# Expert weights loaded in 1 MB halves, and another order of work where the second block begins

## The chip, the cores and the metric

The kernel runs on one core of a Trainium2 chip. The metric is device time in microseconds of one execution; lower is better. Inputs and outputs are fp32.

## The reference

Two blocks follow each other on 256 tokens of width 1024. The first ends in a mixture of 32 experts, of which each token uses two; the second is two layers, each of which begins with an RMS norm and a wide projection. What matters here:

```python
def expert_block(args):                       # for each of the 32 experts
    xb, e = args
    return (jax.nn.silu(xb @ w1[e]) * (xb @ w3[e])) @ w2[e]   # 1024 -> 512 -> 1024
...
x = x + g2[:, None] * y                       # y: weighted sum over experts, by token
x = rmsnorm(x, final_g)                       # end of the first block
...
for layer in range(2):                        # second block
    h = rmsnorm_2(x, norm_w)
    proj = jnp.matmul(h, w_in)                # then attention, retention, mLSTM
    ...
    x = x + jnp.matmul(y, w_out)
return rmsnorm_2(x, final_norm_w)
```

## The kernel before

**Experts.** Experts are worked in 16 pairs (`NP`). The two experts of a pair sit side by side on TensorE, each in 64 of its columns, so one pass over a 512-wide row of weights is one matmul of either expert. A pair takes six loads of 2 MB, issued by SP in the order w1, w1, w3, w3, w2, w2. They go round eight slots of 2 MB (`ring` has six, `more` has two). SP waits before each load until its slot is free: a slot of w1 or w3 is given back by `s_up`, which TensorE raises after all eight rows of the pair's w1 or w3; a slot of w2 by `s_down` after the whole w2. TensorE, in `experts_pe`, waits for whole loads (`arrival`). Per pair it multiplies w1 (L924), w3 (L924), gathers tokens for the next pairs (L881), transposes the weights of tokens and the gated product (L888, L937), adds the pair before to the sum (`scatter_pe`, L901), and multiplies w2 in two halves of 512 columns (L953). ScalarE and VectorE split each result of w2 into a rounded part `ygH` (L1000) and the rest `ygL` (L1055); after the last pair VectorE adds the sum to `xT` (`add_dve`, L1030).

**The second block.** Its weights come as 44 units of 1 MB (22 a layer; one of them, `U_ROWS`, of 512 KB), in four places `raw0` to `raw3`. A unit is multiplied as three fp32r products: ScalarE rounds it to `hi` (L1228), VectorE makes `lo = raw - hi` (L1234), and the input x is split likewise into `HH` (ScalarE, L1674) and `HL` (VectorE, L1971). Each product is HH·hi, HL·hi, HH·lo (L1288). `PIECES` lists the parts of the units in the order of splitting; `high(l, u, i)` and `low(l, u, i)` work it off up to part i of unit u. The first two units of a layer are multiplied together, row by row of the eight rows k (`pair`), each row as soon as its split is there; after row 5 and after row 6 TensorE sums squares for two norms (`stats`, L1318, from squares by ScalarE, L1685 and L1687). The norms' roots and reciprocals (L1582, L1989 to L1999) then stand before everything that reads the projections (L2009 on).

**Order.** Every engine's order is the order in which the code is written; there is no scheduler. Units 0 to 3 and the late constants are issued by SP behind the last expert load, each when its slot is free. A branch for tokens beyond 64 an expert (`overflow`) stands between the experts and the second block; it isn't taken.

Of the kernel before, what the change touches and what calls it, by code (L numbers as in the profile page):

```python
# [32 lines left out]
for _n, _w in (("ident", 128), ("ones", 128), ("one", 256), ("iota", 64), ("low", 128), ("iotam", 32), ("bd", 128), ("negd", 384),  # L33
# [16 lines left out]
PIECES = ([(u, i) for i in range(4) for u in (0, 1)] + [(U_ROWS, 0)] + [(u, i) for u in range(3, U_OUT) for i in range(2)]  # L50
          + [(u, i) for v in (18, 20) for i in range(2) for u in (v, v + 1)])
POOLED = tuple(n for n, (u, i) in enumerate(PIECES) if i == 1 and u in (4, 7, 10, 13))


def build(nc, p, out):
    pe, act, dve, pool, sp = nc.tensor, nc.scalar, nc.vector, nc.gpsimd, nc.sync
    with ExitStack() as ctx:
# [77 lines left out]
        for e in range(0, NE, 2):  # L135
            stream += [piece(p[w][x]) for w in ("expert_w1", "expert_w3") for x in (e, e + 1)]
            stream += [p["expert_w2"][x].rearrange("p (k n) -> p k n", k=4) for x in (e, e + 1)]
# [3 lines left out]
        turns_of = [[n for n in range(len(stream)) if slot_of[n] == i] for i in range(NS)]  # L141
        s_ring = [sem(f"s_ring{i}") for i in range(NS)]

# [9 lines left out]
        def arrival(n):  # L153
            return s_ring[slot_of[n]], 16 * (turns_of[slot_of[n]].index(n) + 1)
# [6 lines left out]
        s_mod, s_mrow, s_fma, s_turn, s_modc, s_half = (sem("s_" + n) for n in ("mod", "mrow", "fma", "turn", "modc", "half"))  # L161
        s_spl, s_proj, s_fill, s_xp, s_cv, s_conv, s_gv, s_ln, s_lnroot, s_sig, s_a, s_aa, s_lru = (
            sem("s_" + n) for n in ("spl", "proj", "fill", "xp", "cv", "conv", "gv", "ln", "lnroot", "sig", "a", "aa", "lru"))
        s_gr, s_gu, s_scan, s_sgu, s_xres = (sem("s_" + n) for n in ("gr", "gu", "scan", "sgu", "xres"))
# [54 lines left out]
        def freed(n):  # L219
# [9 lines left out]
            return (s_up, 2 * q + 1 + r // 2) if r < 4 else (s_down, 2 * q + 2)  # L229
# [8 lines left out]
        def first_sp():  # L238
# [3 lines left out]
            for n in range(FIRST):  # L242
# [4 lines left out]
                if n == ADA[3]:  # L247
                    sp.dma_start(place(W_IN[0])[:, 4:8, :], stream[W_IN[0]][:, 4:8, :]).then_inc(s_half, 16)
# [3 lines left out]

        def stream_sp(first, last):
            for n in range(first, last):
                held = [m for m in turns_of[slot_of[n]] if m < n]
                if held:
                    sp.wait_ge(*freed(held[-1]))
                elif slot_of[n] == 7:
                    sp.wait_ge(s_proj, 18)
                sp.dma_start(place(n), stream[n]).then_inc(s_ring[slot_of[n]], 16)  # L260

# [65 lines left out]
        def mixer_pe():  # L327
# [50 lines left out]
            pe.wait_ge(s_half, 16)  # L378
# [86 lines left out]
            project(14, W_OUT[0], 0, yT, y_ready, 0, (s_gu, 2))  # L465
            project(15, W_OUT[0], 2, yT, None, 0, (s_gu, 4))
# [35 lines left out]
        def mixer_act():  # L502
# [52 lines left out]
            for u, dst, signal in ((8, gr, s_gr), (10, gu, s_gu)):  # L555
# [71 lines left out]
        def mixer_dve():  # L627
# [80 lines left out]
            for j in range(4):  # L708
# [5 lines left out]
                dve.wait_ge(s_gu, j + 1)  # L714
# [191 lines left out]
        def experts_pe(first, last):  # L906
            for n in range(first, last):
                q, o = n // 2, 128 * (n % 2)

                for i in range(2):  # L910
# [33 lines left out]
                for a in range(2):  # L944
# [4 lines left out]
                    for f in range(4):  # L949
                        for x in range(2):  # L950
                            if a == 0 and f == 0:
                                pe.wait_ge(*arrival(at[x]))
                            t = pe.matmul(bank[5 + a][64 * x:64 * x + 64, :], aT[:, f, 64 * x:64 * x + 64],  # L953
                                          place(at[x])[:, f, 512 * a:512 * a + 512], start=f == 0, stop=f == 3)
# [3 lines left out]
        def gathered_act(q, a, ps):  # L958
            act.wait_ge(s_gath, 4 * q + 2 * a + 1)
            if q >= 2:  # L960
                act.wait_ge(s_up, 4 * (q - 1))
# [5 lines left out]
        def gathered_dve(q, a, ps):  # L967
            dve.wait_ge(s_gath, 4 * q + 2 * a + 2)
            if q >= 2:
                dve.wait_ge(s_up, 4 * (q - 1))  # L970
# [5 lines left out]
        def experts_act(first, last, high=None):  # L976
            for n in range(first, last):
                act.wait_ge(s_up, 2 * n + 1)
# [15 lines left out]
                for a in range(2):  # L994
# [6 lines left out]
                    if n == NP - 1:  # L1001
                        high(0, 1, 2 * a + 1)
# [30 lines left out]
        def experts_dve(first, last, low=None):  # L1033
            for n in range(first, last):
# [3 lines left out]
                dve.wait_ge(s_up, 2 * n + 2)  # L1038
# [13 lines left out]
                for a in range(2):  # L1052
# [4 lines left out]
                    if n == NP - 1 and a == 0:  # L1057
                        low(0, 1, 1)
# [1132 lines left out]
        for a in range(4):  # L2191
            add_dve(a)
# [117 lines left out]
```

## Time and profile before

| | |
|---|---|
| device time, median of 3 runs | 954.54 us (954.53 to 956.31) |
| the profiled execution | 954.87 us, its span 953.1 us |
| PE busy | 878.9 us, 92% of the span |
| DMA in the span | 291.42 MB, mean 306 GB/s |
| HBM read | 289.52 MB |
| q1 (all weight loads) | 24480 packets, 74.1% of 16 engines' span |
| expert loads | 96 of 2 MB, 27 us from issue to landing |

The page divides the span into 40 slices. In slices 8 to 24 DMA moves 403 to 428 GB/s; from slice 25 on it moves 45 to 221. PE is busy nearly everywhere, and VectorE and ScalarE, light in the experts, rise to 7 or 8 tenths and 5 to 7 tenths behind them. Busy shares alone don't say which of them sets the pace; the chain of waits does.

### The profile page before, as it was taken

How to read it: one execution, taken by the hardware profiler on the slowest of the kernel's cores; microseconds unless marked ns; L12 is line 12 of the kernel's file. 1: busy time of each engine (PE TensorE's matmuls, PEld its weight loads, DVE VectorE, ACT ScalarE, POOL GpSimd, SP SyncE). 2: the span in 40 equal slices, each digit the busy share in tenths (PEclk: the TensorE clock that was granted, in tenths of full speed). 3: DMA queues.
4: the chain of work that ended last, by engine and by line, in shares of the span. 5: the costliest groups of instructions: out<-in, count | busy, mean ns of one | idle time of the engine just before them, and what ended most of it. 6: DMA issues, size and time to landing. Idle time of an engine off the chain costs nothing.

```text
span 953.1 us, 12730 instructions
## 1 busy us (share of the span) xinstructions
PE 878.9 (92%) x5340; PEld 579.0 (61%) x5340; DVE 415.0 (44%) x780; ACT 310.3 (33%) x564; POOL 36.7 (4%) x23
## 2 busy tenths in 40 slices
PE   4999999999989898898988988889999998999995
PEld 2668874444334443344433433788889898888985
DVE  4096951111111111011110110687887858788772
ACT  3362141111011111111111111657256565725662
POOL 0001000000000000000000000011110001111000
PEclk9899999999999999999999999999999999999998
DMA  9999889999999999999999999152333236233321
GB/s 381 425 427 428 321 313 403 428 428 427 428 427 428 427 427 428 427 428 426 428 428 428 428 427 423 45 221 89 134 133 133 99 145 221 89 134 133 133 89 45
DMA packets 24538, 291.42 MB, mean 306 GB/s; under 512 B 2720, under 2 KB 2976, under 8 KB 4000
## 3 DMA queue, kind: packets, MB, share of 16 engines
q1 hardware_dynamic: 24480, 290.58, 74.1%
q8 instruction: 44, 0.72, 0.3%
q14 instruction: 14, 0.11, 0.0%
HBM read 289.52 MB, written 1.05 MB: 305 GB/s over the span
## 4 chain that ended last, share of the span: by engine, by line
PE 54%; DMA 25%; DVE 14%; ACT 5%; issue 2%; SPq 1%; DVEq 0%; ACTq 0%
DMA ring<-in_expert_w 19%; PE bank L1288 15%; PE bank L924 14%; PE bank L953 7%; PE bank L345 4%; DMA more<-in_expert_w 3%; DVE lo L1234 3%; PE bank L881 2%; DMA ring<-in_ada_w 2%; DVE X L315 2%; PE bank L901 2%; PE bank L360 2%; PE bank L387 1%; PE bank L1318 1%; ACT hi L1228 1%
## 5 line engine op out<-in xcount | busy, mean ns | idle before, releaser
L924 PE MATMUL bank<-ring,xg 128*64 128x512 f32 x768 | 236.9, 607 | 21.5 <-DMA ring<-in_expert_w 20.5
L924 PEld LDWEIGHTS bank<-ring,xg 128*64 128x64 f32 x768 | 73.3, 140 | 142.7 <-issue 109.0
L1288 PE MATMUL bank<-HH,hi 128*128 128x256 f32 x432 | 129.1, 299 | 11.4 <-DVE lo L1234 9.1
L924 PE MATMUL bank<-more,xg 128*64 128x512 f32 x256 | 117.1, 608 | 8.1 <-DMA more<-in_expert_w 8.1
L1288 PE MATMUL bank<-HL,hi 128*128 128x256 f32 x432 | 123.3, 286 | 0.0
L1288 PE MATMUL bank<-HH,lo 128*128 128x256 f32 x432 | 123.2, 285 | 0.0
L1042 DVE TENSOR_TENSOR X<-X,bank 128x512 f32<-128x512 f32 x16 | 11.0, 687 | 237.5 <-PE bank L924 237.5
L953 PE MATMUL bank<-ring,X 128*64 128x512 f32 x384 | 113.3, 595 | 0.0
L1288 PEld LDWEIGHTS bank<-HH,hi 128*128 128x128 f32 x432 | 83.9, 194 | 18.6 <-issue 10.2
L1234 DVE TENSOR_TENSOR lo<-raw,hi 128x1024 fp32r<-128x1024 f32 (+1 forms) x86 | 93.1, 1118 | 2.3 <-ACT hi L1228 2.3
L1228 ACT ACTIVATE hi<-raw 128x1024 fp32r<-128x1024 f32 (+1 forms) x94 | 87.0, 975 | 11.2 <-DMA raw<-in_units 11.1
L1288 PEld LDWEIGHTS bank<-HL,hi 128*128 128x128 f32 x432 | 84.0, 195 | 1.1 <-issue 1.0
L1288 PEld LDWEIGHTS bank<-HH,lo 128*128 128x128 f32 x432 | 83.9, 194 | 0.0
L1055 DVE SCALAR_TENSOR_TENSOR ygL<-bank,small,ygH 128x512 fp32r<-128x512 f32 x32 | 24.0, 751 | 131.7 <-ACT ygH L1000 131.7
L924 PEld LDWEIGHTS bank<-more,xg 128*64 128x64 f32 x256 | 34.9, 140 | 49.8 <-issue 37.3
L953 PEld LDWEIGHTS bank<-ring,X 128*64 128x64 f32 x384 | 34.5, 137 | 49.6 <-issue 48.0
L1000 ACT ACTIVATE ygH<-bank,small 128x512 fp32r<-128x512 f32 x32 | 22.0, 687 | 119.1 <-PE bank L953 119.1
L964 ACT ACTIVATE xg<-bank,modc 128x256 f32<-128x256 f32 x32 | 13.4, 470 | 140.4 <-PE bank L881 140.4
L953 PE MATMUL bank<-more,X 128*64 128x512 f32 x128 | 56.6, 595 | 0.7 <-ACT X L993 0.7
L1234 POOL TENSOR_TENSOR lo<-raw,hi 128x1024 fp32r<-128x1024 f32 x8 | 22.5, 2816 | 739.6 <-ACT hi L1228 739.6
L981 ACT ACTIVATE X<-bank 128x512 f32<-128x512 f32 x16 | 9.6, 597 | 110.6 <-PE bank L924 110.6
L1288 PE MATMUL bank<-YH,hi 128*128 128x256 f32 x128 | 37.6, 294 | 2.8 <-DVE lo L1234 2.4
(334 smaller groups left out, 1457.2 us busy)
## 6 DMA issues: line engine op xcount, KB each, us to landing
ring<-in_expert_w SPq DMA_DIRECT2D x72, 2048.0 KB, 27.1
more<-in_expert_w SPq DMA_DIRECT2D x24, 2048.0 KB, 26.9
raw<-in_units SPq DMA_DIRECT2D x42, 1024.0 KB, 4.8
ring<-in_ada_w SPq DMA_DIRECT2D x10, 2048.0 KB, 20.0
ring<-in_w_in SPq DMA_DIRECT2D x3, 2048.0 KB, 33.4
more<-in_ada_w SPq DMA_DIRECT2D x2, 2048.0 KB, 28.1
ring<-in_w_out SPq DMA_DIRECT2D x2, 2048.0 KB, 19.6
ring<-in_w_in SPq DMA_DIRECT2D x2, 1024.0 KB, 22.1
```

The lines of the kernel that those rows point to most:

```text
L315: dve.scalar_tensor_tensor(a, w[:, k, :], cs[:, k:k + 1], a, ALU.mult, ALU.add).then_inc(s_fma, 1)
L345: t = pe.matmul(ps[:, T * j:T * j + T], w[:, k, 128 * (first + j):128 * (first + j) + 128], rhs[:, k, :], start=k == 0, stop=k == 7)
L360: t = pe.matmul(bank[4 + u][:, T * j:T * j + T], w[:, k, 256 * u + 128 * j:256 * u + 128 * j + 128], hT[:, k, :], start=k == 0 and j == 0, ...
L881: t = pe.matmul(ps[:, T * k:T * k + T], part(ht[:, i, d:d + 128]), part(Pm[q % 2][:, i, :]), start=j == 0, stop=j == 3)
L901: t = pe.matmul(bank[ACC[a]][:, T * k:T * k + T], part(y[:, d:d + 128]), part(PT[n % 2][:, :]), start=n == 0 and k == 0 and j == 0, stop=n ...
L924: t = pe.matmul(bank[3 + i][64 * x:64 * x + 64, :], xg[q % 2][:, k, o + 64 * x:o + 64 * x + 64], place(at[x])[:, k, :], start=k == 0, stop ...
L953: t = pe.matmul(bank[5 + a][64 * x:64 * x + 64, :], aT[:, f, 64 * x:64 * x + 64], place(at[x])[:, f, 512 * a:512 * a + 512], start=f == 0, ...
L1000: act.activation(part(ygH[:, 512 * a:512 * a + 512]), bank[5 + a][:, :], ACT.Copy, scale=weight[n % 2]).then_inc(s_ygh, 1)
L1055: dve.scalar_tensor_tensor(part(ygL[:, h]), bank[5 + a][:, :], weight[n % 2], ygH[:, h], ALU.mult, ALU.subtract).then_inc(s_ygl, 1)
L1228: act.activation(part(hi), src, ACT.Copy).then_inc(s_hi, 1)
L1234: e.tensor_tensor(part(lo), src, hi, ALU.subtract).then_inc(signal, 1)
L1288: t = pe.matmul(ps[:, T * j:T * j + T], part(st), part(mv), start=first and a == 0, stop=last and a == 2, skip_group_check=True)
```

## The change

1. Each expert load is cut into two halves of 1 MB, four of the eight rows each (for w2: one half of the 512-column halves, for which w2 is laid out anew on the host). The halves of a pair's two experts are issued alternately: a0, b0, a1, b1. Each half has its own semaphore, TensorE waits for it alone, and raises `s_up` after each four rows and `s_down` after each half of w2, so each half slot is given back by itself.
2. Rows 0 and 1 of units 0 and 1 of the first layer are no longer split. They are multiplied once in plain fp32, raw weights by `yT`, a scaled copy of x.
3. No split of a unit is made between the last evictions of the experts. The additions to `xT`, the splits of x and the splits of the units' rows 2 to 7 are interleaved row by row (`residual_act`, `residual_dve`), ahead of the branch; the splits of x's rows 0 and 1 come last. The squares are made behind all that.

The core of the diff:

```diff
+PIECES = [(l, u, i) for l in range(2) for u, i in
+          [(u, i) for i in range(0 if l else 1, 4) for u in (0, 1)] + ...
-        def freed(n):
+        def freed(n, half=1):
-            return (s_up, 2 * q + 1 + r // 2) if r < 4 else (s_down, 2 * q + 2)
+            return (s_up, 4 * q + 1 + 2 * (r // 2) + half) if r < 4 else (s_down, 2 * q + 1 + half)
+        def experts_sp(first, last):
+            for n in range(first, last):
+                for i in range(3):
+                    for half in range(2):
+                        for m in (first_load(n) + 2 * i, first_load(n) + 2 * i + 1):
+                            slot_free(m, half)
+                            h = slice(4 * half, 4 * half + 4)
+                            sp.dma_start(place(m)[:, h, :], stream[m][:, h, :]).then_inc((s_more if half else s_ring)[slot_of[m]], 16)
...
-                            if k == 0:
-                                pe.wait_ge(*arrival(at[x]))
+                            if k % 4 == 0:
+                                pe.wait_ge(*arrival(at[x], k // 4))
-                    t.then_inc(s_up, 1)
+                        if k % 4 == 3:
+                            t.then_inc(s_up, 1)
...
-                    if n == NP - 1:
-                        high(0, 1, 2 * a + 1)
...
-                    if n == NP - 1 and a == 0:
-                        low(0, 1, 1)
...
+            def whole(l, u, k):
+                return l == 0 and u < 2 and k < 2
+            def whole_of(k):
+                return act.activation(yT[:, k, :], xT[:, k, :], ACT.Copy, scale=gw[:, k:k + 1])
+            def residual_act():
+                act.wait_ge(s_gw, 1)
+                act.wait_ge(s_down, 2 * NP)
+                high(0, 1, 1)
+                act.wait_ge(s_add, 2)
+                for k in range(2):
+                    whole_of(k).then_inc(s_fin, 1)
+                for k in range(2, 8, 2):
+                    act.wait_ge(s_add, k + 2)
+                    x_high(0, k)
+                    x_high(0, k + 1)
+                    if k < 6:
+                        high(0, 1, k // 2 + 1)
+                x_high(0, 0)
+                x_high(0, 1)
+            def residual_dve():
+                add_dve(0)
+                for k in range(2, 8, 2):
+                    add_dve(k // 2)
+                    low(0, 1, k // 2)
+                    x_low(0, k)
+                    x_low(0, k + 1)
+                x_low(0, 0)
+                x_low(0, 1)
...
+                    if whole(l, u, k):
+                        return pe.matmul(ps[:, T * j:T * j + T], v3(raw[U % 4][:, :], 8)[:, k, 128 * j:128 * j + 128], yT[:, k, :], ...)
...
-                    x_high(0, k)
-                    x_high(0, k + 1)
                     act.activation(squares[:, k:k + 2, :], xT[:, k:k + 2, :], ACT.Square).then_inc(s_sqx, 1)
```

On SP's queue the loads of pair 0 stood like this before, each with the semaphore that it waits for:

```order
L260 DMA ring<-in_expert_w1 128x4096 [waits s_fma]
L260 DMA more<-in_expert_w1 128x4096 [waits s_fma]
L260 DMA ring<-in_expert_w3 128x4096 [waits s_proj]
L260 DMA ring<-in_expert_w3 128x4096 [waits s_fma]
L260 DMA more<-in_expert_w2 128x4096 [waits s_proj]
L260 DMA ring<-in_expert_w2 128x4096 [waits s_proj]
```

In the changed kernel the same place, and the first loads of pair 1 behind the read of `longest`:

```order
L280 DMA ring<-in_expert_w1 128x2048 [waits s_fma]
L280 DMA more<-in_expert_w1 128x2048 [waits s_fma]
L280 DMA ring<-in_expert_w1 128x2048 [waits s_fma]
L280 DMA more<-in_expert_w1 128x2048 [waits s_fma]
L280 DMA ring<-in_expert_w3 128x2048 [waits s_proj]
...
L2248 TENSOR_LOAD longest [waits s_pos]
L2248 ISA x2
L280 DMA ring<-in_expert_w1 128x2048 [waits s_mod] x4
L280 DMA ring<-in_expert_w3 128x2048 [waits s_up]
```

Every load became two of half the width, and the second half of the first expert now stands behind the first half of the second.

On ScalarE, from the last results of the experts (`bank5`, `bank6`) on, before:

```order
L1000 ACTIVATE ygH<-bank5,small 128x512
L1228 ACTIVATE hi0<-raw0 128x512
L1228 ACTIVATE hi1<-raw1 128x512
L1228 ACTIVATE hi0<-raw0 128x512
L1228 ACTIVATE hi1<-raw1 128x512
L1000 ACTIVATE ygH<-bank6,small 128x512
```

And behind the branch, where the squares are made, before:

```order
L1674 ACTIVATE HH<-xT,small 128x256 x2
L1685 ACTIVATE scr<-xT 128x512
L1674 ACTIVATE HH<-xT,small 128x256 x2
L1685 ACTIVATE scr<-xT 128x512
L1674 ACTIVATE HH<-xT,small 128x256 x2
L1685 ACTIVATE scr<-xT 128x512
L1674 ACTIVATE HH<-xT,small 128x256 x2
L1685 ACTIVATE scr<-xT 128x512
L1687 ACTIVATE scr<-xT,cols 128x256 x8
L1228 ACTIVATE hi2<-raw2 128x1024
L1582 ACT_TABLE_LOAD
L1582 ACTIVATE rt<-bank7,small 128x256
```

In the changed kernel the same stretch behind the branch:

```order
L1759 ACTIVATE scr<-xT 128x512 x4
L1761 ACTIVATE scr<-xT,cols 128x256 x8
L1250 ACTIVATE hi2<-raw2 128x1024
L1666 ACT_TABLE_LOAD
L1666 ACTIVATE rt<-bank7,small 128x256
```

The splits of x went ahead of the branch, and the squares (`scr<-xT`), once between them, stand behind all of them.

On VectorE, from the last result of the experts to the branch, in the changed kernel (before, eight additions followed each other there, and the four `lo` of rows 0 to 3 stood between the two `ygL`):

```order
L1074 SCALAR_TENSOR_TENSOR ygL<-bank6,small,ygH 128x512
L1049 SCALAR_TENSOR_TENSOR xT<-bank7,modc,xT 128x256 x2
L1049 SCALAR_TENSOR_TENSOR xT<-bank0,modc,xT 128x256 x2
L1256 TENSOR_TENSOR lo0<-raw0,hi0 128x512
L1256 TENSOR_TENSOR lo1<-raw1,hi1 128x512
L1283 SCALAR_TENSOR_TENSOR HL<-xT,small,HH 128x256 x2
L1049 SCALAR_TENSOR_TENSOR xT<-bank1,modc,xT 128x256 x2
L1256 TENSOR_TENSOR lo0<-raw0,hi0 128x512
L1256 TENSOR_TENSOR lo1<-raw1,hi1 128x512
L1283 SCALAR_TENSOR_TENSOR HL<-xT,small,HH 128x256 x2
```

Additions, splits of units and splits of x now take turns.

## Rows read from the trace of the kernel before

**Rows 1.** The page: slices; one rate is the mean of 23.8 us.

```profile
GB/s 381 425 427 428 321 313 403 428 428 427 428 427 428 427 427 428 427 428 426 428 428 428 428 427 423 45 221 89 134 133 133 99 145 221 89 134 133 133 89 45
```

**Rows 2.** Windows: stretch, length, busy us per engine, granted clock, DMA share, GB/s.

```profile
152.00:156.00 4.00, 4.00 (x22) 1.65 (x20) 0.00 (x0) 0.01 (x1) 0.00 (x0) 1.00 0.96 307
156.00:566.00 410.00, 384.25 (x1933) 165.37 (x1931) 57.66 (x103) 55.62 (x116) 0.00 (x0) 0.99 1.01 428
590.00:595.00 5.00, 5.00 (x27) 1.96 (x27) 0.12 (x1) 0.84 (x2) 0.00 (x0) 1.00 1.02 420
603.00:604.00 1.00, 1.00 (x6) 1.00 (x6) 1.00 (x3) 1.00 (x4) 0.00 (x0) 0.50 0.00 0
624.00:630.00 6.00, 5.46 (x44) 5.05 (x43) 5.83 (x11) 2.87 (x4) 1.17 (x1) 1.00 1.02 430
```

**Rows 3.** SP's issues in order of time; x4 spans from first to last.

```profile
126.37 25.36 SPq L260 DMA_DIRECT2D ring<-in_expert_w  x4
```

**Rows 4.** The chain that ended last: start us, us, what.

```profile
144.29 13.95 PE bank L924 x64
...
547.53 30.93 DMA ring<-in_expert_w
578.51 8.68 PE bank L924 x30
...
590.53 7.04 PE bank L953 x32
...
602.65 10.20 PE bank L1288 x72
612.84 3.45 PE bank L1318 x16
616.30 1.43 PE bank L1288 x12
```

**Rows 5.** PE in order of time; in brackets the idle time before and its releaser.

```profile
568.72 6.65 PE L924 MATMUL bank<-ring,xg 128*64 128x512 f32 x29 [1.28 <-DMA ring<-in_expert_w]
578.51 1.11 PE L924 MATMUL bank<-ring,xg 128*64 128x512 f32 x1 [2.70 <-DMA ring<-in_expert_w]
602.65 0.58 PE L1288 MATMUL bank<-HH,hi 128*128 128x256 f32 x1 [2.31 <-DVE HL L1971]
```

**Rows 6.** The issues of units 0 to 3 (L2184), from issue to landing.

```profile
L2184 SPq DMA_DIRECT2D raw<-in_units x4: 328/328/431, 566.6 to 587.2; - x4
DMA to landing us min/median/max: 9.8/17.8/24.1
```

**Rows 7.** ScalarE in order of time.

```profile
598.18 2.18 ACT L1228 ACTIVATE hi<-raw 128x512 fp32r<-128x512 f32 x4
600.45 0.91 ACT L1674 ACTIVATE HH<-xT,small 128x256 fp32r<-128x256 f32 x2
601.27 0.61 ACT L1685 ACTIVATE scr<-xT 128x512 f32<-128x512 f32 x1
605.74 3.29 ACT L1687 ACTIVATE scr<-xT,cols 128x256 f32<-128x256 f32 x8
608.94 1.04 ACT L1228 ACTIVATE hi<-raw 128x1024 fp32r<-128x1024 f32 x1
610.00 1.28 ACT L1582 ACT_TABLE_LOAD   x1
616.33 0.47 ACT L1582 ACTIVATE rt<-bank,small 128x256 f32<-128x256 f32 x1 [5.05 <-PE bank L1318]
```

**Rows 8.** VectorE in order of time.

```profile
598.98 3.22 DVE L1030 SCALAR_TENSOR_TENSOR xT<-bank,modc,xT 128x256 f32<-128x256 f32 x8
605.75 2.49 DVE L1234 TENSOR_TENSOR lo<-raw,hi 128x512 fp32r<-128x512 f32 x4
616.84 1.75 DVE L1989 RECIPROCAL rstd<-rt 128x256 f32<-128x256 f32 x1 [5.58 <-ACT rt L1582]
621.22 0.42 DVE L1994 TENSOR_TENSOR rs<-rs,bank 128x256 f32<-128x256 f32 x1 [2.17 <-PE bank L1318]
```

More of the change, by code:

```diff
@@ L136, in build @@
             stream += [piece(p[w][x]) for w in ("expert_w1", "expert_w3") for x in (e, e + 1)]
-            stream += [p["expert_w2"][x].rearrange("p (k n) -> p k n", k=4) for x in (e, e + 1)]
+            stream += [p["expert_w2"][x].rearrange("p (k n) -> p k n", k=8) for x in (e, e + 1)]
         slot_of = [3, 2, 0, 4, 5, 1, 6, 3, 2, 4, 5, 0, 6, 1, 2, 3, 4, 5]
@@ L142, in build @@
         s_ring = [sem(f"s_ring{i}") for i in range(NS)]
+        s_more = [sem(f"s_more{i}") for i in range(NS)]
         def unit_place(U):
@@ L151, in unit_arrival, with arrival @@
             return s_ring[U % 4], 16 * (len(turns_of[U % 4]) + U // 4 + 1)
-        def arrival(n):
-            return s_ring[slot_of[n]], 16 * (turns_of[slot_of[n]].index(n) + 1)
+        def arrival(n, half=0):
+            i = slot_of[n]
+            if half:
+                return s_more[i], 16 * ([m for m in turns_of[i] if m >= 18 or m == W_IN[0]].index(n) + 1)
+            return s_ring[i], 16 * (turns_of[i].index(n) + 1)
         s_cols, s_x, s_cst, s_late, s_b1, s_out = (sem("s_" + n) for n in ("cols", "x", "cst", "late", "b1", "out"))
@@ L960, in gathered_act @@
             if q >= 2:
-                act.wait_ge(s_up, 4 * (q - 1))
+                act.wait_ge(s_up, 8 * (q - 1))
             for x in range(2):
@@ L974, in gathered_dve, with experts_act @@
             t.then_inc(s_xg1, 1)
-        def experts_act(first, last, high=None):
+        def experts_act(first, last):
             for n in range(first, last):
-                act.wait_ge(s_up, 2 * n + 1)
+                act.wait_ge(s_up, 4 * n + 2)
                 if n:
@@ L1031, in add_dve, with experts_dve @@
                                          xT[:, m, :], ALU.mult, ALU.add).then_inc(s_add, 1)
-        def experts_dve(first, last, low=None):
+        def experts_dve(first, last):
             for n in range(first, last):
@@ L1282, in products @@
                     hi, lo = (YH, YL) if u >= U_OUT else (HH, HL)
+                    if whole(l, u, k):
+                        return pe.matmul(ps[:, T * j:T * j + T], v3(raw[U % 4][:, :], 8)[:, k, 128 * j:128 * j + 128], yT[:, k, :],
+                                         start=first, stop=last, skip_group_check=True)
                     for a, (x, y) in enumerate(((wh, hi), (wh, lo), (wl, hi))):
@@ L2017, in residual @@
                                       ALU.add).then_inc(s_xo, 1)
-                for k in range(8):
-                    x_low(0, k)
                 for l in range(2):
@@ L2187, in build @@
         experts_pe(1, NP)
-        experts_act(1, NP, high)
-        experts_dve(1, NP, low)
+        experts_act(1, NP)
+        experts_dve(1, NP)
         scatter_pe(NP - 1)
-        for a in range(4):
-            add_dve(a)
-        overflow(length)
+        residual_act()
+        residual_dve()
+        overflow(length, again)
         second_sp()
```

138 lines of the change are left out of this document (76 added, 62 removed).

## The prediction

> **What bounds the kernel now.** I read the page's slices first. Through the experts DMA runs at 427 to 428 GB/s without a break [rows 1], so there the bytes set the pace: 192 half loads or 96 whole ones, it is the same 201 MB, and nothing that frees a slot earlier speeds up a queue that is never empty. Next the windows: from 156 to 566 us the rate is 428 [rows 2], and only the stretch before, 152 to 156, has a hole in it. Then the chain of waits, at the end of that stream: it hangs on a DMA that lands at 578.46, which is the last pair's w3, and from there runs through engines alone [rows 4]. I call that instant L. Behind it come TensorE on w3, VectorE's product, TensorE on w2, which ends at D = 597.57 (590.53 + 7.04), 19.1 us after L. Then a wait: TensorE stands idle 2.31 us for the split of x [rows 5] and starts the second block at 602.65, D + 5.1. Last I read the engines in order of time between D and 625, to see what comes ready when [rows 7, 8]: VectorE's instruction L1994 at 621.22, D + 23.65, is where the norms' chain picks up the second sum of squares, and all projections of the layer are read behind it.
>
> So the change can act in four places: the hole at 152, the pace of the stream, L to D, and D to L1994. I take the far rest as moved along unchanged, since both TensorE's and VectorE's work start from there together and no later instruction is altered in kind.
>
> **1. The hole at 152.** TensorE begins pair 0 at 144.29 and takes 13.95 us for w1 and w3 together, so 7.0 for w1 and 3.5 for half of it [rows 4]. SP's fourth load of the group at 126.37 waits for all of w1 and is issued at about 151.4 (126.37 + 25.36, less its own 0.33) [rows 3]. The queue has meanwhile run dry: 307 GB/s instead of 428 over 4 us is (1 − 307/428) × 4 = 1.13 us lost [rows 2]. With halves the same slot's first half is free at 144.29 + 3.5 = 147.8, 3.6 us earlier and before the queue is dry. The hole closes: −1.2 us for everything behind. It can't give more, as the stream is full from there on. Pair 0's own halves are queued a0, b0, a1, b1, so a1 waits for b's slot though its own is free; but those loads are early for a pair that starts at 144, and I count it nothing (bound 0 to +0.5).
>
> **2. The pace of the stream.** 96 more DMAs are issued and each partition's run shrinks from 16 KB to 8 KB. The trace of before has no 1 MB expert load, but units are such loads. Queued one behind another they move 420 GB/s in 590 to 595 and 430 in 624 to 630; whole loads do 428 [rows 2]. Such short windows scatter by a few GB/s. By the lower one the stream of 201 MB, 471 us at 428, would take 1.9% more, +9.0 us; by the upper one nothing (and −0.5% can't be excluded, −2 us, though I see no reason for it). I take 0.6%, +2.8 us, nearer to no cost since the mean of the two windows is 425. It applies to nearly the whole stream and comes in full at L.
>
> The Trainium skill speaks against this edit (DMA: Bandwidth & Descriptors, section Bandwidth): that section gives 341 GB/s for a transfer of 1 MB and 425 for 16 MB, with the advice to batch to at least 1 MiB, and a floor that comes to about 10.5 ns for each packet. By its packet figure eight more packets an engine and load would be 84 ns, over 96 loads an estimate of +8 us, and the sum would come out near 953.5. Its figure of 341 is for a transfer with nothing queued behind it; the two windows above don't bear it out for queued ones.
>
> **3. From L to D.** Before, TensorE waits for both whole loads of w3 and then needs 8.68 us for it, since after an idle of 2.70 us its first matmuls take 1.11 us instead of 0.59 [rows 5]: the lower of the clock's two levels, 1.2 GHz, which the window at 603, behind the other idle of 2.31 us, reads as 0.50 of 2.4 GHz [rows 2]. A w3 at full clock takes 6.9, as the other row shows (29 in 6.65 us behind an idle of 1.28). With halves the first four rows land one step of 2 MB earlier, 2.10/428 = 4.9 us before L, and are done 3.45 us later, 1.4 us before L; the second half starts at L and is done at L + 3.45, at full clock as an idle of 1.4 us is like the 1.28 of the row. Gain 8.68 − 3.45 = 5.2 us. What follows is unchanged: 587.19 to 590.53 for product, transposes and the pair before, 3.35 us. So w2 starts at L + 6.8. Is its data there? Its halves follow in the stream at L + 4.9 and L + 9.8. The first half of w2 takes 3.5 us, L + 6.8 to L + 10.3, so the second one is just in time (0.5 us to spare), and D falls at L + 13.8. Before it was L + 19.1. Sum −5.25 us. This is the surest term; what could eat it is the second half of w2 landing late, 0 to +1, or a low clock in those 10 us, up to +3.4 (3.45 us of work doubled).
>
> What is late next is the units. Unit 0 is issued at 566.6 and lands 24.1 us later, at 590.7, L + 12.3; unit 3 at 587.2 + 9.8 = 597.0, L + 18.5 [rows 6]. Unit 1 lies 2.45 us behind unit 0, at about L + 14.8, that is 1.0 us behind the new D. ScalarE needs it at D + 1.1, behind `ygH` and the split of unit 0. It fits, barely; if it slips, it costs its own slip on rows 2 and 3 and not on the end of the chain (below). Row 0 and 1 need it raw at D + 2.8.
>
> **4. From D to L1994.** Pitches from one start to the next, a little under the durations since an engine overlaps the next instruction: `hi` 0.52 (half unit), HH 0.41, squares 0.52, L1687 0.40, `hi` of a whole unit 1.05 [rows 7]; additions and HL 0.40, `lo` 0.62 [rows 8]. VectorE: `ygL` until D + 1.4 as before, two additions until 2.2. ScalarE then makes `yT` rows 0 and 1 and TensorE starts at D + 2.7, not D + 5.1. Its own work changes little: eight plain fp32 products at 3.45/8 = 0.43 us each replace 24 of 0.12, as eight `stats` products take 3.45 and twelve fp32r products 1.43 [rows 4], so +0.56; but the 2.31 us idle that put the clock down goes (lower level, 0.50 at 603; 10.20 us for 72 products against 6 × 1.43 = 8.6, so −1.6). TensorE alone would be through its second `stats` at D + 20.2 instead of D + 23.6.
>
> ScalarE decides instead. Following both engines by turns: x rows 2, 3 split by D + 3.9, rows 4, 5 by 6.7, unit rows 6, 7 by 7.7, x rows 6, 7 by 9.5 (VectorE's additions hold them: it is at 8.7 with the last), rows 0, 1 by 10.4; squares until 12.4, the eight L1687 until 15.6, `hi` of unit 2 until 16.6, the table load 1.28 until 17.9, which before lay idle-covered at 610.0, then the root 0.47 until 18.4. VectorE's reciprocal of 1.75 and a product bring L1994 to D + 20.6. TensorE's squares sum is ready at D + 15.4 and 20.2, just ahead. So L1994 moves from D + 23.65 to D + 20.6: −3.0 us. Splitting at nothing: the three unit-row splits on VectorE (0.62 each, six of them) lie in turns with ScalarE and TensorE's rows, since TensorE reaches row 2 at D + 6.2 and HL of it is there at 4.7; row 4 at 9.1 against 7.5; row 6 at 15.4 against 10.4. The new wait for HL rows 0 and 1 (queued behind it: all later tiles) is over at D + 11.6, long before D + 21.7. The branch now stands directly before TensorE's first product; before, the 2.31 us wait covered it; if it costs all of it, ScalarE's chain still ends at 20.6 and TensorE's at 22.5, so +1.9. Bounds of this term: −3.4 (TensorE alone) to −1.1.
>
> **Sum.** −1.2 + 2.8 − 5.25 − 3.0 = −6.65 us. Against the profiled execution's own 954.87 us that gives 948.2; it stands 0.33 above the median of 954.54, so on the median 947.9. I say 948.2.
>
> **Rivals.**
> A. The pace costs nothing: term 2 is 0, time 954.87 − 9.45 = 945.4. For it the window at 430, against it the one at 420. Chance 0.17.
> B. The front of the second block gives nothing, because the branch, a late unit 1 or ScalarE's later squares hold L1994 where it was, or the low clock takes half of term 3: 948.2 + 3.0 = 951.2. For it that every step there has under 1 us to spare. Chance 0.13.
> C. The pace costs the 1.9% of the lower window, +9.0, which leaves −0.4: 954.4, no change. Chance 0.07.
> D. Slower than before: the small loads cost the stream more than the other terms give. It decides from 9.45/96 = 98 ns a load, or 2.0% of pace, on; a short unit load takes 4.8 us alone where its bytes need 2.45, so if only 6% of that excess of 2.3 us stayed uncovered at each of 96 more issues, 0.14 × 96 = +13 us, 958.7. Against it that queued units run at 420 or better. Chance 0.05.
> The forecast itself, 946 to 951, has 0.58.
>
> Faster by over 0.2% (below 952.6; 0.2% is about what a measurement can tell) 0.88, within it 0.07, slower 0.05. The range takes in A and B and reaches part of the way to C: 944.5 to 953.0.
>
> **What would show it.** Windows over 160 to 560 must read between 425 and 428 GB/s; 420 is C, less is D. The hole at 152 to 156 must be filled. The last w3 must show half its products behind a wait, at 0.43 us a pair, and L to D must be near 13.8. TensorE's idle before its first product on `yT` must be under 0.5 us. L1994 must stand near D + 20.6, with the table load now directly before the root; if TensorE's `stats` ends after ScalarE's root instead, my order of the two is wrong. The forecast falls if the stream's rate falls by over 1%, or if D moves by less than 4 us against L.

## The result and the profile after

The changed kernel is slower: 961.84 us (median of 7, 960.31 to 964.11) against 957.07 (median of 7, 954.53 to 960.03), ratio 1.0064 with a 95% interval of [1.0047, 1.0081]. (The ratio is the recorded one and not the quotient of the two medians, 1.0050; of the seven runs of the kernel before, three are those of its first page, 954.5 to 956.3, and the other four took 957.1 to 960.0.) The forecast was 948.2 with 944.5 to 953.0. The two profiled executions lie 5.5 us apart: 960.39 us with a span of 958.6, against 954.87 and 953.1; it is these two traces that the differences below are taken from. (The median of the kernel before differs from chip to chip, 954.5 to 957.1; each ratio below is against runs on its own chip.)

The page after: slices and packets.

```profile
GB/s 381 426 426 427 283 343 423 421 420 420 422 420 420 421 420 423 420 422 420 421 421 421 422 420 420 88 203 105 132 122 144 90 153 212 97 133 132 133 89 44
DMA packets 38364, 291.43 MB, mean 304 GB/s; under 512 B 4257, under 2 KB 4513, under 8 KB 5537
```

Where [rows 1] had 427 and 428, it reads 420 to 423. The windows after:

```profile
152.00:156.00 4.00, 4.00 (x22) 1.68 (x20) 0.00 (x0) 0.00 (x0) 0.00 (x0) 1.00 0.99 414
156.00:566.00 410.00, 379.06 (x1921) 165.68 (x1918) 57.60 (x103) 55.70 (x116) 0.00 (x0) 1.00 1.01 421
598.00:602.00 4.00, 3.21 (x20) 2.02 (x16) 2.39 (x6) 2.54 (x6) 0.00 (x0) 1.00 1.04 431
602.00:604.00 2.00, 0.00 (x0) 0.00 (x0) 2.00 (x5) 1.93 (x5) 0.00 (x0) 1.00 0.64 270
604.00:606.00 2.00, 0.00 (x0) 0.00 (x0) 2.00 (x5) 1.26 (x3) 0.00 (x0) 0.60 0.34 131
```

Against [rows 2] the hole at 152 is filled (414 for 307), and the 410 us behind it run at 421 GB/s for 428. In 602 to 606 TensorE does nothing at all while the other two engines are busy; the granted clock falls within that idle, from 1.00 to a mean of 0.60. The chain of waits after, from the last landing of w3 on (L is now 584.79):

```profile
556.97 27.82 DMA ring<-in_expert_w
584.79 0.04 issue
584.84 3.66 PE bank L944 x14
...
591.83 7.04 PE bank L974 x32
598.87 0.02 issue
...
601.18 0.92 ACT yT L1280 x2
602.10 4.64 issue
606.74 5.90 PE bank L1363 x16
612.64 5.74 PE bank L1370 x48
618.39 3.45 PE bank L1400 x16
...
626.77 0.42 DVE rs L2063
```

It answers to [rows 4]. L moved from 578.46 to 584.79, +6.3. D moved only from 597.57 to 598.87: L to D is 14.1 for 19.1. The instruction that was L1994 is L2063 now, at D + 27.9 for D + 23.65. From there to the end of the span it is 331.8 us, for 331.9. So the account closes: +6.33 at L, −5.03 from L to D and +4.25 from there to L2063 are +5.55, for 5.5 between the spans.

The new thing is the piece of 4.64 us that is called issue: `yT` is there at 602.10, TensorE begins at 606.74, and no instruction or semaphore that the profile records stands between. The order of time on TensorE says the same:

```profile
584.84 0.64 PE L944 MATMUL bank<-ring,xg 128*64 128x512 f32 x1 [2.43 <-DMA ring<-in_expert_w]
606.74 5.90 PE L1363 MATMUL bank<-yT,raw 128*128 128x256 f32 x16 [5.11 <-issue]
```

In the first of these rows the second half of w3 waits 2.43 us for its data and then starts at full clock (0.64 us, where [rows 5] has 1.11 behind an idle of 2.70). In the second, TensorE has just passed the branch `overflow`, and stands for 5.11 us, 4.64 of them behind both rows of `yT`. That the branch isn't taken, as said above, means that its body is skipped: what TensorE does next lies behind that body in the code.

One thing does fall into that idle. The profile counts the packets that bring instructions on queues of their own. The page after has 44 of them on q8, of 16 KB each, and the page of e3 (below), a kernel without the branch, has 42:

```profile
q8 instruction: 44, 0.72, 0.3%
```

```profile
q8 instruction: 42, 0.69, 0.3%
```

One of the 44 starts in 604.0 to 604.2, with 34.4% of 16 engines' 0.2 us, which is 1.1 us of one engine; in the run e5, below, it starts in 602.7 to 602.9:

```profile
q8 instruction: 1, 0.02, 34.4%
```

```profile
q8 instruction: 1, 0.02, 34.2%
```

### The profile page after: what moved, and what is told of

The parts are those of the page before. It is cut to its first block, busy times and chain, and to the rows that moved or that the text cites. A ratio compares the mean times of both kernels' runs of the same rounds, so it can differ in the third digit from the quotient of the medians.

```text
span 958.6 us, 12824 instructions
## 1 busy us (share of the span) xinstructions
PE 876.6 (91%) x5332; PEld 580.3 (61%) x5332; DVE 413.5 (43%) x778; ACT 310.9 (32%) x564; POOL 36.7 (4%) x23
## 2 busy tenths in 40 slices
DMA packets 38364, 291.43 MB, mean 304 GB/s; under 512 B 4257, under 2 KB 4513, under 8 KB 5537
## 4 chain that ended last, share of the span: by engine, by line
PE 45%; DMA 33%; DVE 13%; ACT 5%; issue 2%; SPq 1%; DVEq 0%; ACTq 0%
DMA ring<-in_expert_w 23%; PE bank L1370 15%; PE bank L944 10%; DMA more<-in_expert_w 8%; PE bank L974 4%; PE bank L365 4%; DVE lo L1256 3%; DMA ring<-in_ada_w 2%; DVE X L335 2%; PE bank L380 1%; PE bank L407 1%; PE bank L901 1%; PE bank L1400 1%; ACT hi L1250 1%; PE bank L295 1%
## 5 line engine op out<-in xcount | busy, mean ns | idle before, releaser
L944 PE MATMUL bank<-ring,xg 128*64 128x512 f32 x768 | 233.9, 596 | 27.0 <-DMA ring<-in_expert_w 25.8
L1370 PE MATMUL bank<-HH,hi 128*128 128x256 f32 x424 | 126.2, 298 | 9.1 <-DVE lo L1256 9.1
L1370 PE MATMUL bank<-HL,hi 128*128 128x256 f32 x424 | 120.5, 284 | 0.0
L1370 PE MATMUL bank<-HH,lo 128*128 128x256 f32 x424 | 120.4, 284 | 0.0
L1370 PEld LDWEIGHTS bank<-HH,hi 128*128 128x128 f32 x424 | 81.7, 193 | 16.1 <-issue 10.2
L1370 PEld LDWEIGHTS bank<-HL,hi 128*128 128x128 f32 x424 | 81.8, 193 | 1.1 <-issue 1.0
L1370 PEld LDWEIGHTS bank<-HH,lo 128*128 128x128 f32 x424 | 81.8, 193 | 0.0
## 6 DMA issues: line engine op xcount, KB each, us to landing
ring<-in_ada_w SPq DMA_DIRECT2D x10, 2048.0 KB, 20.7
ring<-in_w_out SPq DMA_DIRECT2D x2, 2048.0 KB, 20.6
```

The lines of the kernel that those rows point to most:

```text
L1370: t = pe.matmul(ps[:, T * j:T * j + T], part(st), part(mv), start=first and a == 0, stop=last and a == 2, skip_group_check=True)
```

## The experiments

After the result there are two theories on each of two questions. For the pace: (P1) each partition's run of 8 KB instead of 16 KB costs rate, or (P2) the count of DMAs does. For the front: (F1) the branch before the first product costs TensorE the idle of 5.1 us, or (F2) something else behind `yT` does (the plain fp32 products, the lower clock, ScalarE's order, a late unit). The expectations call F1 the branch theory, and the fetch of the code behind the branch the refetch; of F2 they weigh the plain products, as the fp32 theory.

**e1: the halves alone.** The front of the second block is as in the kernel before.

```diff
+        def experts_sp(first, last):
...
+                    for half in range(2):
+                        for m in (first_load(n) + 2 * i, first_load(n) + 2 * i + 1):
+                            slot_free(m, half)
...
```

> The expert loads in halves, the front of the second block as before. The changed kernel measured 1.0064 of before. Three theories on where its time went. Pace: halves slow the stream from 428 to 421 GB/s, so the last w3 lands 6 to 7 us later than before (578.5 before, 584.8 in the changed kernel), and the tail from there to the end of w2 shrinks from 19.1 to 14.1 us. All three theories expect that here: w2 ends about 1.3 us later than before. Branch theory: TensorE's idle of 5.1 us before its first product of the second block, in the changed kernel, is a refetch of instructions behind the branch whose DMA stands behind the weight stream, which now ends later. Then here too TensorE is held beyond the split of x: first product at D + 6 to D + 8 where before it was D + 5.1, and the time is 957 to 959. fp32 theory: the idle belongs to the plain fp32 products (raw weights and yT); then here the first product comes at D + 5.1 as before, and the time is 955.8 to 956.5.

Measured: 961.21 us (9 runs), ratio 1.0059 [1.0043, 1.0075], 421 GB/s from 156 to 566. Its chain at the end of the experts:

```profile
577.53 22.55 DMA raw<-in_units
600.08 0.02 issue
600.10 0.64 ACT hi L1247
...
600.76 1.90 DVE lo L1253 x3
602.66 0.66 DVE ygL L1074
...
607.65 0.37 issue
608.02 11.11 PE bank L1307 x72
```

The halves alone give a loss of the same size, by another path behind L than the changed kernel's. The rate is the changed kernel's, and L is at 585.18. What the halves gain in the tail is in part eaten by the lower clock (L to D is 15.7 us here: behind an idle of 2.71 us w3's last products run at the lower level) and mostly by a wait that part 1 creates: the splits of the units stand between the last evictions, the unit that ScalarE needs lands only at 600.08, and `ygL`, which TensorE's last additions need, stands queued behind them. Part 3 of the change removes just that. Neither theory on the front had this wait in its expectation, so the run doesn't decide between them; the piece called issue is 0.37 us here.

**e2: the front alone.** Whole loads as before, parts 2 and 3 as in the change.

```diff
...
-        experts_sp(1, NP)
+        stream_sp(first_load(1), len(stream))
...
```

> The new order at the front of the second block (rows 0 and 1 in plain fp32, splits in turns), the expert loads whole as before. Stream at 428 GB/s, D at 597.6 as before. Branch theory: the stream behind the experts ends near 600, so the refetch behind the branch is over sooner, and TensorE starts at D + 3 to D + 5; time between 951.5 and 954.5. fp32 theory: the idle of 5.1 us stays whole, TensorE starts at D + 7.9, and the time is 957 or more. Prediction's own view (no such idle): D + 2.7 and 951.5.

Measured: 953.96 us (10), ratio 0.9985 [0.9967, 1.0002], 427 GB/s. D = 595.81 (in this execution w3 took 7.09 us behind an idle of 2.71, for 8.68 behind 2.70 before, so 1.6 of the 1.8 us by which D is earlier are the clock's and not the edit's), and the second sum of squares is picked up at 618.43, D + 22.6. Its chain:

```profile
598.69 1.35 PE bank L1344 x5
600.03 1.73 issue
601.77 2.53 PE bank L1344 x11
```

Here the stall is 1.7 us, and comes behind five products instead of ahead of the first. The front gives 1.0 us of its 3 in this trace (D + 22.6 for D + 23.65), and the time can't be told from that of the kernel before.

**e3: the change without the branch.** It leaves out the work for tokens beyond 64 an expert, of which there are none in this data.

```diff
-        overflow(length, again)
```

> The changed kernel without the branch for more than 64 tokens an expert (the part of the computation left out: the overflow of tokens beyond 64 an expert, which these inputs don't have). Branch theory: TensorE's idle of 5.1 us before its first product of the second block falls to under 0.6 us, and the kernel takes 4 to 5 us less than the changed kernel, 955.5 to 956.5 in its terms of 960.4. fp32 theory: the idle stays at 5 us and the time at 960.

Measured: 954.22 us (10), ratio 0.9982 [0.9967, 0.9997]; beside the changed kernel's 1.0064 that is 0.8%, some 8 us. The rate is 421 GB/s as in the changed kernel. (In this one trace L itself comes 3.0 us later than there, at 587.80, as 140 to 152 moved 240 GB/s for 343; so the two spans differ by only 4.0.) The chain of waits:

```profile
601.88 0.02 issue
...
604.19 0.52 ACT yT L1280
604.71 0.04 issue
604.75 3.72 PE bank L1363 x16
608.48 5.75 PE bank L1370 x48
...
622.61 0.42 DVE rs L2063
```

The stall is gone. D is 601.88, the first product starts at D + 2.9, the eight products (16 matmuls in the records) take 3.72 us for 5.90, and L2063 stands at D + 20.7. No instruction packet of q8 starts between 586.6 and 610.0. F1 holds: the plain products are still there, and the idle is not. (The edit takes out the branch together with the code that it skips, so it doesn't part the two.)

**e4: the late constants issued behind the branch.** If the fetch of TensorE's code waits behind transfers in flight, less traffic should shorten the stall.

```diff
-        sp.wait_ge(*freed(max(turns_of[6])))
-        sp.dma_start(late[:, :], p["cst"][:, EARLY:]).then_inc(s_late, 16)
...
         overflow(length, again)
+        sp.wait_ge(*freed(max(turns_of[6])))
+        sp.dma_start(late[:, :], p["cst"][:, EARLY:]).then_inc(s_late, 16)
```

> The changed kernel with the 1.5 MB load of late constants issued behind the branch instead of ahead of it, so that the stream behind the experts ends 3.7 us earlier. Branch theory with its fetch behind the stream: TensorE's idle before its first product shrinks by 2 to 3.7 us, and so does the time. Branch theory with a cost of its own that doesn't depend on the stream: the idle stays at 5.1 us and the time at 960. fp32 theory: the same as the latter.

Measured: 961.17 us (7), ratio 1.0060 [1.0043, 1.0078], idle 5.0. SP's issue of the late constants, in the changed kernel and in this one:

```profile
588.89 0.43 SPq L2254 DMA_DIRECT2D late<-in_cst  x1
```

```profile
589.39 0.33 SPq L2261 DMA_DIRECT2D late<-in_cst  x1
```

It moved by 0.5 us, and L is 0.3 us later in this trace too. SP waits for nothing at the branch and passes it as soon as its own code reaches it, so this run tested nothing.

**e5: the same, with a wait.** Units 2 and 3 and the late constants are issued only when VectorE has made its second split of x, that of row 3.

```diff
+        place_units((0, 1))
...
         overflow(length, again)
+        sp.wait_ge(s_hl, 2)
+        place_units((2, 3))
+        sp.wait_ge(*freed(max(turns_of[6])))
+        sp.dma_start(late[:, :], p["cst"][:, EARLY:]).then_inc(s_late, 16)
```

> The changed kernel with units 2 and 3 and the late constants issued only after VectorE's second split of x, so that nothing but units 0 and 1 is in flight when TensorE passes the branch (the run before this one moved only the late load, and SP issued it at the same time as before, so it tested nothing). If the refetch behind the branch stands behind the weight stream, TensorE's idle before its first fp32 product falls from 5.1 us to 1 to 2 us and the kernel takes 3 to 4 us less than the changed kernel: ratio to before 1.002. If the branch costs what it costs whatever the stream does, the idle stays at 5 us and the ratio at 1.006.

Measured: 958.79 us (10), ratio 1.0032 [1.0013, 1.0051]. Windows and waits:

```profile
598.00:602.00 4.00, 3.58 (x22) 1.71 (x19) 1.32 (x3) 1.73 (x3) 0.00 (x0) 1.00 0.01 4
602.00:604.00 2.00, 0.97 (x8) 0.77 (x7) 2.00 (x6) 1.48 (x4) 0.00 (x0) 1.00 0.03 8
```

```profile
PE bank L1363 <- issue: 2.5, 1, 2.5
```

With 4 and 8 GB/s around the branch instead of 431 and 270 the idle is 2.5 us instead of 5.1. In this trace L2063 stands at D + 24.7 (D = 600.21), for D + 27.9; the products on `yT` still take 5.38 us, for 5.90. (L to D is 15.8 here for 14.1, as the last 14 matmuls of w3 take 5.36 us for 3.66; so the span, 956.8, gains less than the front does.) Half the stall came from what else was being moved.

The instruction packet shows which half. In the changed kernel it starts 2.5 us after TensorE's last matmul has ended (at 601.63); here it starts 0.2 us before that end (602.97). It takes 1.1 us in both, and the first product on `yT` starts 1.6 and 1.5 us after its end. (e7 and e8 below show the same pair: 2.6 us after the last matmul's end, and 0.2 before it.) So the loads in flight lengthened the time until the packet started, and not the packet or what follows it.

**e6: each expert load as two DMAs of 64 partitions**, in the kernel before: twice the DMAs, runs still of 16 KB.

```diff
-                sp.dma_start(place(n), stream[n]).then_inc(s_ring[slot_of[n]], 16)
...
+                    sp.dma_start(place(n)[0:64], stream[n][0:64]).then_inc(s_ring[slot_of[n]], 16)
+                    sp.dma_start(place(n)[64:128], stream[n][64:128]).then_inc(s_ring[slot_of[n]], 16)
```

> The kernel before, with each expert load issued as two DMAs of 64 partitions instead of one of 128: as many expert DMAs as in the changed kernel (192 of 1 MB), but runs of 16 KB as before. If the pace hangs on the number of DMAs, the windows from 156 to 566 us read 421 GB/s and the time grows by 6 to 7 us. If it hangs on the length of a partition's run, they read 427 to 428 and the time is that of before within 1 us.

Measured: 1401.99 us (4), ratio 1.4610 [1.4511, 1.4709].

```profile
156.00:540.00 384.00, 231.70 (x880) 86.46 (x878) 28.18 (x52) 26.35 (x55) 0.00 (x0) 0.79 1.01 214
```

The rate is half, with DMA busy throughout. It shows what a load into 64 partitions costs, and nothing about the count.

**e7: halves only for the last pair**, whose tail is what the halves shorten.

```diff
+        HALVED = 18 + 6 * (NP - 1)
...
+                if first_load(n) < HALVED:
+                    stream_sp(first_load(n), first_load(n + 1))
+                    continue
```

> The changed kernel with halves for the last pair of experts alone; the other 15 pairs are loaded whole as before. If the loss is the pace, it goes: 427 GB/s from 156 to 540, the last w3 lands at 578 to 579, w2 ends 14.1 us later. Then TensorE's idle at the branch (5.1 us in the changed kernel, 1.7 us in the kernel with the front alone) decides: with 5.1 us the time is 953 to 954, with 1.7 us 950. If the stream was not the loss, the time stays near 960.

Measured: 956.14 us (10), ratio 0.9996 [0.9975, 1.0017].

```profile
156.00:540.00 384.00, 359.66 (x1816) 156.55 (x1814) 55.04 (x99) 52.58 (x110) 0.00 (x0) 0.99 1.01 427
```

```profile
571.65 14.24 PE bank L948 x64
...
599.50 4.80 issue
604.30 5.08 PE bank L1367 x16
```

The pace is back. TensorE now enters the last pair late, behind the pair before it with its whole loads, and goes through w1 and w3 in 14.24 us without a wait. D is 596.27, 1.3 us ahead of the kernel before, and the stall of 4.8 us takes more than that back: L2067, the former L1994, is at 623.50 for 621.22 in this trace.

**e8: e7 and e5 together.**

```diff
+        HALVED = 18 + 6 * (NP - 1)
...
+        sp.wait_ge(s_hl, 2)
+        place_units((2, 3))
```

> Halves for the last pair alone, and units 2 and 3 and the late constants issued behind VectorE's second split of x. If the refetch stands behind the weight stream: TensorE's idle at the branch 1 to 2 us, 949 to 950, faster than both kernels. If the branch's cost doesn't hang on the stream: the same as halves for the last pair with the issues left where they are.

Measured: 952.83 us (10), ratio 0.9968 [0.9947, 0.9989]: faster than both kernels, though less so than the 949 to 950 expected. Its chain:

```profile
597.84 1.98 issue
599.82 3.69 PE bank L1367 x16
```

4.80 has become 1.98, and the products run at full clock (3.69 us), though TensorE's idle before them is 2.45 us as in e5, where they took 5.38.

**e9: halves for the last four pairs, and the wait of e5.**

```diff
-        HALVED = 18 + 6 * (NP - 1)
+        HALVED = 18 + 6 * (NP - 4)
```

> Halves for the last four pairs of experts, the others whole; units 2 and 3 and the late constants behind VectorE's second split of x. With halves for the last pair alone TensorE came to it late (its w1 and w3 ran without a wait), since the pair before had waited 2.7 us for whole loads and restarted at the lower clock; so w2 ended at 594.6. If that is so, four pairs let TensorE catch up: w3's second half waits for its load again, w2 ends at 592 to 593, the idle at the branch is 2.5 us, and the time is 1.5 to 2.5 us below that kernel, near 949; ratio 0.994. If TensorE's lateness isn't what held it, the time is the same as with the last pair alone.

Measured: 952.09 us (6), ratio 0.9965 [0.9945, 0.9986].

```profile
156.00:490.00 334.00, 314.71 (x1584) 135.89 (x1582) 49.03 (x88) 46.16 (x96) 0.00 (x0) 0.98 1.01 427
540.00:566.00 26.00, 22.46 (x106) 8.87 (x108) 2.62 (x4) 3.05 (x6) 0.00 (x0) 1.00 1.01 420
```

Both rates stand in one kernel: 427 where loads are whole, 420 where they are halves. L to D is 14.1 us again (580.17 to 594.25), but L comes 1.7 us later than before, which the expectation of 949 had left out. Against e8 no difference can be told.

**e10: the changed kernel with half the DMAs.** One DMA of 2 MB carries the same half of both experts: 96 DMAs, runs of 8 KB. Slots are dealt out so that the two lie side by side.

```diff
-                        for m in (first_load(n) + 2 * i, first_load(n) + 2 * i + 1):
...
-                            sp.dma_start(place(m)[:, h, :], stream[m][:, h, :]).then_inc((s_more if half else s_ring)[slot_of[m]], 16)
...
+                        dst = ring[:, s:s + 2, h] if s < 6 else more[:, 0:2, h]
+                        src = p[("expert_w1", "expert_w3", "expert_w2")[i]][2 * n:2 * n + 2].rearrange("a p c -> p a c")[:, :, h]
+                        sp.dma_start(dst, src).then_inc((s_more if half else s_ring)[s], 16)
```

> The changed kernel with the same halves of a pair's two experts brought in by one DMA (2 MB, runs of 8 KB, slots side by side): as many expert DMAs as before, 96, and runs as short as in the changed kernel. If the pace hangs on the length of a run, the window from 156 to 540 reads 421 GB/s and the time is that of the changed kernel, ratio 1.006. If it hangs on the number of DMAs, it reads 427 and the kernel gains 6 us on the changed one, ratio near 1.000.

Measured: 965.24 us (2), ratio 1.0108 [1.0089, 1.0127].

```profile
156.00:540.00 384.00, 344.98 (x1792) 151.72 (x1790) 54.32 (x98) 51.96 (x109) 0.00 (x0) 1.00 1.01 421
DMA packets 36827, 291.42 MB, mean 303 GB/s; under 512 B 2720, under 2 KB 2976, under 8 KB 4000
```

As many DMAs as the kernel before, and 421 GB/s as in the changed one. P1 holds and P2 falls. The time is longer than the changed kernel's, against the expectation of 1.006, as L comes at 589.4, 4.6 us later; that is lost ahead of the steady stretch, where 110 to 140 moves 303 GB/s for 383. The packets say what changed: 36827 for 24538 is 12289 more, which is 96 loads times 128 partitions, each run in two pieces now. The changed kernel has another 1537 on top, all under 512 bytes (4257 for 2720), which is 16 for each of its 96 more DMAs; they cost no rate that can be seen.

**e11: e2 with the wait of e5.**

```diff
+        sp.wait_ge(s_hl, 2)
+        place_units((2, 3))
```

> The new front with whole loads (which stalled 1.7 us behind its fifth plain product), and units 2 and 3 and the late constants behind VectorE's second split of x. If the refetch stands behind the stream, TensorE is held less: idle under 1 us in all, and the time falls by about 1 us against the front alone, ratio 0.9975. If not, no change, 0.9985.

Measured: 954.12 us (12), ratio 0.9993 [0.9983, 1.0004], where 0.9975 was expected; the stall is 1.45 us for 1.73. No gain can be told: in e2 little of the stream was left, 81 GB/s in 598 to 602.

**e12: the kernel before without its branch.** It leaves out the work for tokens beyond 64 an expert.

```diff
-        overflow(length)
```

> The kernel before without the branch (left out: the overflow of tokens beyond 64 an expert, which these inputs don't have). The branch theory says that the refetch was there before too and was covered by TensorE's wait of 2.3 us for the split of x: first product at D + 5.1 as with the branch, no change in time, ratio 0.999 to 1.001. If the branch cost the kernel before anything, its idle of 2.31 us shrinks and the ratio is 0.998 or less.

Measured: 954.32 us (10), ratio 0.9996 [0.9983, 1.0009].

```profile
602.13 0.40 DVE HL L1971
...
602.57 10.39 PE bank L1288 x72
```

TensorE waits 2.31 us for `HL` as in [rows 5]. In the kernel before the branch cost nothing that can be measured; it lay wholly below that wait.

## Why the prediction was wrong, step by step

**Term 1, the hole (−1.2): right.** 307 became 414, 4 × 107/428 = 1.0 us. (The slices just ahead changed as well, from 321 and 313 to 283 and 343; over 80 to 156 the changed kernel moved some 0.4 MB more, which is 0.9 us of the stream.)

**Term 2, the pace (+2.8): the step that failed first.** Its mechanism and its bounds were named (−2 to +9.0); the value was taken between two windows of 5 and 6 us that differ by 2.4% from each other, as if their mean meant something. Measured, 421 for 428 over 410 us is 1.7%, 410 × 7/421 = +6.8 us, and some 7 up to L: L moved by 6.3 with the hole's 1.0 taken off. Rival C, the lower window's 1.9%, had the right size. Put as packets it is 7 us × 16 engines / 12288 packets = 9 ns for each additional packet on its engine.

The Trainium skill's figure of about 10.5 ns for a packet (DMA: Bandwidth & Descriptors, section Bandwidth) had given an estimate of +8 us in the prediction. The trace bears it out within 1 us, though that section's 341 GB/s for a transfer of 1 MB does not hold for queued ones, which run at 421.

**Term 3, L to D (−5.25): right in size, with some luck in the clock.** It measured −5.03, with both halves of w3 and w2 as worked out: 3.66 us at full clock, w2's 7.04 without a break. But the idle before w3's second half was 2.43 us, and the forecast had 1.4 and took the full clock from that. In e1 and e5 it was 2.71 and 2.67, the clock fell, and L to D was 15.7 and 15.8: the low clock that the prediction named as what could eat the term took 1.7 us there.

**Term 4, D to L1994 (−3.0): failed, at the clause on the branch.** The prediction said that the branch stood directly before TensorE's first product, gave it no cost in the sum, and bounded its cost by 2.31 us, the idle that had covered it. That is no bound: a wait that covers a stall shows only that the stall is not longer than the wait was there, and says nothing of it in another place with other traffic. The bound also kept the 1.6 us that the term had gained from the clock, though an idle of 2.31 us is just what had put the clock down before. The stall was 5.11 us. It cost twice: the first product stands at D + 7.87 where e3 has it at D + 2.87, 5.0 us; and as the granted clock had fallen in that idle, to a mean of 0.60 in 604 to 606 with 0.50 as the lower level, the products took 5.90 us for the 3.72 of e3, 2.2 more. e3's 20.7 + 5.0 + 2.2 is the 27.9 measured. The rest of the term was right: e3, which has no branch, stands at D + 20.7 for the D + 20.6 of the working, and its root starts at 619.79, D + 17.9, as worked out from ScalarE's turns. Only the order at the very end was another: TensorE's second sum, reckoned at D + 20.2, ends there at D + 20.7, 0.1 us behind VectorE's product on the root's side.

What is shown: taking the branch away removes the stall (e3); moving less beside it halves it (TensorE's idle is 2.45 us in e5 for 5.11 in the changed kernel, and 2.45 in e8 for 5.27 in e7). That TensorE stands for a fetch of the code behind the branch is the reading that fits all of it: an instruction packet of 16 KB lies in the stall of each of the kernels that stand there (the changed one, e4, e5 and e7 to e10), its end always 1.5 to 1.6 us ahead of the first product, and none lies there in e3. The profile doesn't say which engine's code a packet carries, nor what the 1.5 us behind it are. The Trainium skill states that a taken branch whose target isn't on hand forces a DMA fetch before execution goes on (Runtime: NRT & Kernel Launch, section Instruction fetch mechanics). It gives no duration; the trace agrees in kind, with a packet of 1.1 us in an idle of 2.5 to 5.3 us.

What stays open: in e2 and e11 the stall is 1.73 and 1.45 us and comes behind five matmuls, and not ahead of the first. Such a packet lies near it too, and ends 1.4 us before TensorE goes on. Their code differs in length ahead of the branch, which could shift what has been fetched; no run varied that by itself. Nor is it known why ScalarE shows no such stall: in e5 its first instruction behind the branch starts at 610.48, without an idle, while 387 to 436 GB/s are moved.

**The sum.** Forecast −6.65, measured +5.5. Of the 12.15 us between, terms 1 and 2 have 4.7 (+6.3 at L for +1.6), term 3 has 0.2 and term 4 has 7.25. The mechanisms were the forecast's own, C's size for the pace and B's first cause, the branch, for the front, both at once and the second far beyond its bound. Each had been given a chance of its own, and their coming together none. Rival D came nearest to the time, by a price a load that the count of e10 excludes.

**The best version.** Halves where they shorten the end (one pair or four) and the late transfers kept off the branch: 0.9968 [0.9947, 0.9989] and 0.9965 [0.9945, 0.9986]. The interval of e2, with whole loads throughout (0.9967 to 1.0002), overlaps both. An idle of 2.45 and 2.33 us at the branch is left in them.

## What to carry to other kernels

This stream, which never pauses, paid for its additional packets over its whole length: cut loads small only where a latency at the end of the chain is at stake, and leave the others whole. Before moving work onto the first instructions behind a branch, ask what wait has hidden that branch so far; take the wait away and the branch is on the path, and here its cost was twice as large while other transfers ran. An idle that a chain calls issue can be looked up among the instruction packets: a packet inside it points to a fetch. Where a term has measured bounds far apart that apply to half the span, the mean of them is not a forecast; the mechanism has to be priced by itself.

## What the hardware showed that was not expected

- Runs of 8 KB instead of 16 KB in each partition: 421 for 427 to 428 GB/s, the same with 192 DMAs or 96 (e10), and within one kernel (e9).
- A branch on TensorE cost 2.5 us of idle with the queues nearly empty (4 to 8 GB/s) and 5.1 us beside 431 and 270 GB/s; the chain of waits shows it only as issue.
- In that idle lies one instruction packet of 16 KB. It took 1.1 us with or without other loads (e5 and the changed kernel), but started 2.5 us after TensorE's last matmul beside them and 0.2 us before its end without them.
- Idles of nearly one length left the clock up in one execution and down in another: behind 2.70 and 2.71 us w3 took 8.68 us (before) and 7.09 (e2); behind 2.45 us the 16 matmuls on `yT` took 5.38 us (e5) and 3.69 (e8).
- DMAs into 64 of the 128 partitions moved 214 GB/s one behind another, with DMA busy throughout, for 428 into all 128 (e6).
- SP passed the branch long before TensorE did: a DMA written behind it left at 589.39, for 588.89 when written ahead of it, and TensorE's first product behind it started at 606.98 (e4).
